# The experts' down weights issued from GpSimd's DMA queue instead of SyncE's, in a two-block transformer forward pass on one core

## The chip, the cores and the metric

The kernel runs on one NeuronCore of a Trainium2 chip. Times are device microseconds (us) of one launch. The span of a profile runs from the first to the last instruction of the profiled execution.

## The reference

Two transformer blocks of 256 tokens by 1024 features in float32 run one after the other. The first has four layers, each a mixer (forgetting attention, S5, pooling, forgetting attention) and a dense SwiGLU of width 2816. The second has two layers with a hybrid mixer; its first feed-forward is dense, its second is a mixture of eight experts of width 3584, and each token uses two of them:

```python
def swiglu_2(x, wg, wu, wd):
    return (jax.nn.silu(x @ wg) * (x @ wu)) @ wd

def moe_swiglu(x, router, wg, wu, wd):
    t = x.reshape(bsz * s, d)
    top_v, top_i = lax.top_k((t @ router).astype(jnp.float32), TOP_K)
    top_w = jax.nn.softmax(top_v, axis=-1)
    gate = jnp.sum(jax.nn.one_hot(top_i, N_EXPERTS) * top_w[..., None], axis=1)
    for e in range(N_EXPERTS):
        y = y + gate[:, e:e + 1] * swiglu_2(t, wg[e], wu[e], wd[e])
```

The change touches only how the weights of this mixture reach on-chip memory.

## The kernel before

Every engine has a hand-written program, and semaphores join them. SyncE (SP) issues nearly all loads of weights. GpSimd (POOL) does no arithmetic in the layers: it issues small loads of parameters, the last two of which are the scale and shift rows of the final layer norm (L958, 0.5 MB each, one descriptor of 4 KB per partition), after it has waited for version 13 of x (the rows after the last mixer's layer norm).

**The expert stage** runs from 1935 us to the end. It gathers up to 88 tokens for each expert. An expert has 14 chunks of 256 hidden features. A chunk is three pieces of weights: 1 MB of gate, 1 MB of up, 1 MB of down. There are four slots: three in `ring` and one in `arena` (`expert_slot`, L372). In each slot the first 4096 columns hold gate or up weights, the last 2048 the down weights. Gate and up are loaded for two chunks at a time: one DMA of 2 MB puts gate for both into the even slot, a second puts up for both into the odd slot. Such two chunks are called a pair here. A down DMA brings 1 MB for one chunk.

**TensorE's order** (L1743 to L1821) is `gate_up` of chunk c (L1762, 128 matmuls of 64 weight columns and 88 tokens), then `down` of chunk c-1 (L1778, 64 matmuls). Before the `gate_up` of an even slot it waits until both 2 MB DMAs have landed (`ex_loaded`, L1754); before a `down`, for its 1 MB (`ex_down_loaded`, L1771). The first matmul of the `down` that follows an odd slot's `gate_up` gives that pair's gate and up places back (`ex_released`, L1782); the last matmul of a `down` gives that down place back (`ex_down_released`, L1784). Twelve of an expert's chunks run in a hardware loop of three rounds with four chunks each (L1809); between two experts there are the output transposes (L1725), the gather for the next expert (L1710) and the scatter of the last result (L1737).

**SyncE's order** (`expert_chunk`, L534 to L550) is written out: for each chunk in turn, with an even slot first wait for `ex_released` and issue gate and up, then in either case wait for `ex_down_released` of the slot and issue down. All go to one hardware DMA queue, q1 in the profile, which spreads each DMA over the 16 DMA engines. The first four chunks wait instead for the ring slots that the last mixer still uses, and for version 13 of x for the slot in `arena` (`place_free`). POOL's DMAs go to another queue, q0; TensorE's own instructions are fetched in blocks of 16 KB through q8.

In a gate or up DMA a descriptor moves 2 KB (512 columns of float32); in a down DMA it moves 8 KB (two rows of 1024), so each engine has 64 descriptors of a gate or up DMA and 8 of a down DMA.

Of the kernel before, what the change touches and what calls it, by code (L numbers as in the profile page):

```python
# [12 lines left out]
D = 1024  # L13
# [10 lines left out]
N_EXP = 8  # L24
# [11 lines left out]
FC = 256  # L36
NSUB = FC // P
# [5 lines left out]
PASSES = -(-S // CAP)  # L43
# [142 lines left out]
def build(nc, inp, table, out):  # L186
# [3 lines left out]
    with ctx:  # L190
        def sb(name, shape, dt=F32):
            return ctx.enter_context(nc.sbuf_tensor(name, shape, dt))

        def sem(name):
            return ctx.enter_context(nc.semaphore(name))
# [170 lines left out]
        overflow = sb("overflow", [P, 1], I32)  # L366
        M_CH = F_EXP // FC
        M_RING = RING + 1
# [3 lines left out]
        def expert_slot(n):  # L372
            return ring[:, n, :] if n < RING else last_slot
# [19 lines left out]
        def x_at(ver):  # L393

            return (x_part, 4 * (ver - 1)) if 2 <= ver <= 9 else (x_ready, 1 if ver == 1 else ver - 8)
# [27 lines left out]
        ex_down_loaded = [sem(f"expert_down_loaded{i}") for i in range(RING + 1)]  # L423
        ex_released = [sem(f"expert_gate_up_released{i}") for i in range(RING + 1)]
        ex_down_released = [sem(f"expert_down_released{i}") for i in range(RING + 1)]
        rows_loaded = sem("row_vectors_loaded")
        rows_used = sem("row_vectors_used")
        overflow_ready = sem("overflow_flag_ready")
# [19 lines left out]
        def _(sp):  # L448
            t = Tally()
# [78 lines left out]
            def place_free(slot):  # L528
                if slot < RING:
                    sp.wait_ge(released[slot], t.count[f"released{slot}"] + 1)  # L530
                else:
                    sp.wait_ge(*x_at(13))

            def expert_chunk(gate, up, down, f0, first):  # L534

                n = t.up("expert_chunk") - 1
                slot = n % M_RING
                if slot % 2 == 0 and not first:
                    sp.wait_ge(ex_released[slot + 1], t.up(f"ex_released{slot + 1}"))
                if slot % 2 == 0:  # L540
                    for i, w in enumerate((gate, up)):
                        if first:
                            place_free(slot + i)
                        sp.dma_start(expert_slot(slot + i)[:, 0:4096].rearrange("p (k n) -> p k n", n=2 * FC),
                                     w.rearrange("(k p) n -> p k n", p=P)[:, :, bass.ds(f0, 2 * FC)])\
                          .then_inc(ex_loaded[slot], 16)
                if not first:
                    sp.wait_ge(ex_down_released[slot], t.up(f"ex_down_released{slot}"))
                sp.dma_start(expert_slot(slot)[:, 4096:6144].rearrange("p (s n) -> p s n", n=D),
                             down[bass.ds(f0, FC), :].rearrange("(p s) n -> p s n", s=NSUB)).then_inc(ex_down_loaded[slot], 16)  # L550

            def moe_pass(b):
                for e in range(N_EXP):
                    gate, up, down = (inp[k][0, e] for k in ("moe_w_gate_2", "moe_w_up_2", "moe_w_down_2"))
                    first = b == e == 0
                    for c in range(2 if not first else M_RING):
                        expert_chunk(gate, up, down, c * FC, first)
                    done = 0
                    if first:
                        for c in range(M_RING, 2 + M_RING):  # L560
                            expert_chunk(gate, up, down, c * FC, False)
                        done = 1
                    with sp.Fori(0, M_ROUNDS - done) as i:
                        adds = {f"ex_released{j}": 1 for j in range(1, M_RING, 2)}
                        adds.update({f"ex_down_released{j}": 1 for j in range(M_RING)})
                        adds["expert_chunk"] = M_RING
                        t.enter(i, M_ROUNDS - done, adds)
                        for j in range(M_RING):
                            expert_chunk(gate, up, down, i * (M_RING * FC) + (j + 2 + done * M_RING) * FC, False)
                        t.leave()  # L570

            moe_pass(0)
            sp.wait_ge(overflow_ready, 1)
            more = sp.value_load(overflow[0:1, 0:1], min_val=0, max_val=1)
            with sp.If(more > 0):
                for b in range(1, PASSES):
                    moe_pass(b)
# [359 lines left out]
        @block.gpsimd  # L937
        def _(pool):

            pool.wait_ge(x_ready, 1)  # L940
            n = 0
            br, bi = (inp[k][0].rearrange("g p c -> p g c") for k in ("s5_b_re", "s5_b_im"))
            cr, ci = (inp[k][0].rearrange("(k g) c p -> (g c) k p", g=GPT) for k in ("s5_c_re", "s5_c_im"))
            loads = [(b_own[0:64], br), (b_own[64:P], bi), (b_other[0:64], bi), (b_other[64:P], br),
                     (c_in[:, 0, :, 0:64], cr), (c_in[:, 0, :, 64:P], ci)]
            for half in (slice(0, 64), slice(64, P)):
                loads += [(lam_in[0:G5, 0, half], inp["s5_a_re"][0]), (lam_in[0:G5, 1, half], inp["s5_a_im"][0])]
            loads += [(dt5, inp["s5_log_dt"].broadcast_to([P, G5]))]
            for dst, src in loads:
                pool.dma_start(dst, src, allow_slow_non_contiguous=True).then_inc(s5_loaded, 16)  # L950
                n += 16
            assert n == S5_LOADS, n

            pool.dma_start(router.rearrange("p (k e) -> p k e", e=N_EXP),
                           inp["moe_router_2"][0].rearrange("(k p) e -> p k e", p=P)).then_inc(router_loaded, 16)

            def row(k, src):
                pool.dma_start(rowv[:, k, :], src.broadcast_to([P, D])).then_inc(rows_loaded, 16)  # L958
            pool.wait_ge(*x_at(4))
            pool.dma_start(arena[:, LATE_AT:LATE_AT + n_const - n_early], table[:, n_early:n_const]).then_inc(late_loaded, 16)  # L960
            row(0, inp["pool_b"])
            row(1, inp["pool_scale"])
            pool.wait_ge(*x_at(6))
            row(0, inp["final_norm_g"].rearrange("(o d) -> o d", o=1))
            for n, (wn, bn, l) in enumerate((("ln1_w_2", "ln1_b_2", 0), ("ln2_w_2", "ln2_b_2", 0),
                                             ("ln1_w_2", "ln1_b_2", 1), ("ln2_w_2", "ln2_b_2", 1))):
                pool.wait_ge(*x_at(10 + n))
                row(0, inp[wn][l:l + 1, :])
                row(1, inp[bn][l:l + 1, :])


        @block.tensor
        def _(pe):
# [724 lines left out]
            pe.wait_ge(late_loaded, 16)  # L1698
            hybrid(0, turn_z(0))
            tks = [tk for _, tk in turn_z(4)]  # L1700
            ffn(tks[0:2], tks[2:4], (), plain=False)
            hybrid(1, turn_z(0))
# [968 lines left out]
```

## Time and profile before

| | |
|---|---|
| median of 3 runs | 2904.29 us (2901.03 to 2906.14) |
| the profiled execution | 2901.52 us; span 2899.6 us |
| TensorE busy over the span | 2736.8 us, 94% |
| q1 | 606.13 MB |
| mean granted TensorE clock | 0.985 of full |

In the profile PE is TensorE's matmuls, PEld its weight loads (they overlap), SPq the issuing on SyncE's queue. An "idle" in brackets stands in front of the group beside which it is printed; "issue" is idle time for which no semaphore or DMA was found. Line numbers are those of the kernel before.

### The profile page before, as it was taken

Reading aid. Unit: us, or ns where it says so; the run is one execution under the profiler, and the core shown is the slowest. Engines: PE = TensorE matmul, PEld = TensorE weight load, DVE = VectorE, ACT = ScalarE, POOL = GpSimd, SP = SyncE. Lnnn points to the kernel's source line nnn. Section 1 sums busy time; section 2 is a strip of 40 time slices with the busy share of each in tenths; the row PEclk is TensorE's granted clock in tenths of the full one; section 3 lists DMA queues with packets and bytes.
Section 4 is the critical chain, followed back from the end, with each engine's and each line's share of the span. In section 5 each row is a group of like instructions: output and inputs, shape, how many; then the busy total and the mean of one; then the engine's idle time right before and its main releaser. Section 6 shows DMA issues by size and latency. Waiting matters only on the chain.

```text
span 2899.6 us, 79960 instructions
## 1 busy us (share of the span) xinstructions
PE 2736.8 (94%) x37718; PEld 2201.9 (76%) x37718; DVE 957.6 (33%) x1644; ACT 344.5 (12%) x717; POOL 18.5 (1%) x28
## 2 busy tenths in 40 slices
PE   8999998999899999999999999889999999979997
PEld 5677775677687775776657776569899998978987
DVE  1445444445645415544355343540000000000001
ACT  1210022100100003000240001510000000000000
POOL 1000000000000000000000000000000000000000
PEclk9999999999999999999999999999999999999998
DMA  7244413554434433354324543259999999997995
GB/s 223 89 144 141 164 59 118 182 175 158 170 129 139 171 132 110 124 175 146 115 102 148 173 161 130 102 192 384 371 396 377 381 392 366 395 373 281 382 382 209
DMA packets 307917, 620.55 MB, mean 214 GB/s; under 512 B 8886, under 2 KB 126908, under 8 KB 293212
## 3 DMA queue, kind: packets, MB, share of 16 engines
q1 hardware_dynamic: 304688, 606.13, 57.7%
q0 software_dynamic: 2400, 10.09, 1.1%
q8 instruction: 211, 3.46, 0.5%
q10 hardware_dynamic: 588, 0.63, 0.1%
q14 instruction: 30, 0.25, 0.0%
HBM read 615.77 MB, written 1.05 MB: 213 GB/s over the span
## 4 chain that ended last, share of the span: by engine, by line
PE 79%; DVE 9%; DMA 7%; issue 3%; ACT 1%; SPq 1%; DVEq 0%; ACTq 0%
PE ps L1762 19%; PE ps L1028 12%; PE ps L1187 12%; PE ps L1115 9%; PE ps L1778 9%; PE ps L1039 8%; DMA ring<-in_ffn_w_down 6%; PE ps L1677 2%; PE ps L1737 1%; PE ps L1710 1%; DVE arena L1912 1%; DVE ring L1911 1%; DVE arena L1910 1%; DVE arena L1913 1%; DVE arena L2065 1%
## 5 line engine op out<-in xcount | busy, mean ns | idle before, releaser
L1762 PE MATMUL ps<-arena,ring 128*64 128x88 f32 x10752 | 438.8, 240 | 29.7 <-issue 27.9
L1762 PEld LDWEIGHTS ps<-arena,ring 128*64 128x64 f32 x10752 | 423.4, 139 | 39.8 <-issue 37.6
L1115 PE MATMUL ps<-ring,arena 128*128 128x512 f32 x880 | 390.3, 597 | 0.0
L1028 PE MATMUL ps<-xT,ring 128*128 128x256 f32 (+2 forms) x1664 | 363.9, 380 | 2.2 <-DVE xT L1880 1.0
L1028 PEld LDWEIGHTS ps<-xT,ring 128*128 128x128 f32 (+2 forms) x1664 | 312.4, 188 | 55.9 <-issue 9.0
L2591 DVE TENSOR_TENSOR arena<-arena,ps 128x176 f32<-128x176 f32 x112 | 37.8, 338 | 844.6 <-ACT arena L899 844.6
L1115 PEld LDWEIGHTS ps<-ring,arena 128*128 128x128 f32 x880 | 163.2, 190 | 193.2 <-issue 193.1
L1778 PE MATMUL ps<-arena,ring 128*64 128x88 f32 x5376 | 224.0, 239 | 12.4 <-issue 12.4
L1778 PEld LDWEIGHTS ps<-arena,ring 128*64 128x64 f32 x5376 | 214.1, 137 | 13.2 <-issue 13.2
L1187 PEld LDWEIGHTS ps<-xT,ring 128*64 128x64 f32 x2816 | 158.1, 140 | 53.1 <-issue 53.1
L1187 PE MATMUL ps<-xT,ring 128*64 128x128 f32 x2816 | 167.9, 278 | 22.8 <-DVE arena L1997 16.6
L1910 DVE TENSOR_TENSOR arena<-ring 128x1024 f32<-128x1024 f32 x44 | 53.9, 1224 | 361.7 <-DMA ring<-in_ffn_w_down 361.7
L1187 PE MATMUL ps<-arena 128*64 128x128 f32 x2816 | 170.3, 273 | 0.0
L1187 PE MATMUL ps<-arena,ring 128*64 128x128 f32 x2816 | 162.0, 273 | 0.0
L1187 PEld LDWEIGHTS ps<-arena 128*64 128x64 f32 x2816 | 158.4, 137 | 0.0
L1762 PE MATMUL ps<-arena 128*64 128x88 f32 x3584 | 149.9, 239 | 7.2 <-issue 7.2
L1187 PEld LDWEIGHTS ps<-arena,ring 128*64 128x64 f32 x2816 | 156.1, 137 | 0.0
L1762 PEld LDWEIGHTS ps<-arena 128*64 128x64 f32 x3584 | 142.9, 138 | 9.1 <-issue 8.9
L643 ACT ACTIVATE arena<-arena 128x512 f32<-128x512 f32 x55 | 34.7, 630 | 945.7 <-DVE arena L2002 596.5
L899 ACT ACTIVATE arena<-ps 128x176 f32<-128x176 f32 x112 | 35.5, 317 | 824.1 <-PE ps L1762 824.1
L1039 PE MATMUL ps<-ring,xT 128*128 128x512 f32 (+1 forms) x320 | 131.7, 572 | 0.0
L1039 PE MATMUL ps<-ring,arena 128*128 128x512 f32 (+1 forms) x288 | 119.4, 576 | 3.2 <-ACT arena L718 3.2
(443 smaller groups left out, 2294.1 us busy)
## 6 DMA issues: line engine op xcount, KB each, us to landing
ring<-in_moe_w_gate SPq DMA_DIRECT2D x56, 2048.0 KB, 9.8
ring<-in_ffn_w_gate_up SPq DMA_DIRECT2D x88, 1024.0 KB, 7.5
ring<-in_moe_w_down SPq DMA_DIRECT2D x84, 1024.0 KB, 14.5
ring<-in_moe_w_up SPq DMA_DIRECT2D x28, 2048.0 KB, 14.2
arena<-in_moe_w_up SPq DMA_DIRECT2D x28, 2048.0 KB, 14.8
ring<-in_ffn_w_down SPq DMA_DIRECT2D x55, 1024.0 KB, 11.0
arena<-in_moe_w_down SPq DMA_DIRECT2D x28, 1024.0 KB, 10.2
ring<-in_fox_w_in SPq DMA_DIRECT2D x20, 768.0 KB, 6.1
```

The lines of the kernel that those rows point to most:

```text
L643: act.activation(g, g, ACT.Silu).then_inc(silu_ready, 1)
L899: act.activation(silu[:, par, 0:NSUB * CAP], ps[:, par, 0:NSUB * CAP], ACT.Silu).then_inc(silu_ready, 1)
L1028: ins = pe.matmul(o, lhsT=w[:, k, c0:c0 + m], rhs=rhs[:, k, :], start=(k == 0), stop=(k == kt - 1))
L1039: ins = pe.matmul(o, lhsT=lhs[:, k0 + k, i * P:(i + 1) * P], rhs=w[:, k, c0:c0 + n], start=(k == 0), stop=(k == kt - 1))
L1115: return pe.matmul(ps[:, 4 + 2 * i + h, :], lhsT=h_par[:, s * S + i * P:s * S + (i + 1) * P], rhs=w[:, s, h * 512:(h + 1) * 512], start=(c ...
L1187: ins = pe.matmul(o[h], lhsT=w_of[:, u, k, h], rhs=x_of[:, k, :], start=(k == 0), stop=(k == 3))
L1677: ins = pe.matmul(ps[:, b, :], lhsT=mixT[:, k, (b % 2) * P:(b % 2 + 1) * P], rhs=w[:, k, 0:512], start=(k == 2), stop=(k == 7), skip_group ...
L1710: ins = pe.matmul(ps[h, 6 + k // 4, (k % 4) * CAP:(k % 4 + 1) * CAP], lhsT=x[:, i, k * P + h.start:k * P + h.stop], rhs=perm[:, e, i, :], ...
L1762: ins = pe.matmul(ps[h, par, c0:c0 + CAP], lhsT=w[:, k, s, h], rhs=xe[:, k, :], start=(k == 0), stop=(k == KD - 1))
L1778: ins = pe.matmul(o[h], lhsT=w[:, s, m * P + h.start:m * P + h.stop], rhs=hid[:, par, s * CAP:(s + 1) * CAP], start=False, stop=False, ski ...
L1910: then(tt(t3, b22, b12, ALU.subtract))
L2591: dve.tensor_tensor(hid[:, par, 0:NSUB * CAP], silu[:, par, 0:NSUB * CAP], ps[:, par, NSUB * CAP:2 * NSUB * CAP], ALU.mult).then_inc(hid_r ...
```

## The change

SyncE now issues only gate and up. POOL, after its last layer-norm rows, runs a loop of its own over experts and chunks, waits for `ex_down_released` of the slot (not for the first four chunks), and issues the same down DMA with the same semaphore. Every other engine is as before.

```diff
-            def expert_chunk(gate, up, down, f0, first):
+            def expert_chunk(gate, up, f0, first):
...
-                if not first:
-                    sp.wait_ge(ex_down_released[slot], t.up(f"ex_down_released{slot}"))
-                sp.dma_start(expert_slot(slot)[:, 4096:6144].rearrange("p (s n) -> p s n", n=D),
-                             down[bass.ds(f0, FC), :].rearrange("(p s) n -> p s n", s=NSUB)).then_inc(ex_down_loaded[slot], 16)
...
@@ the end of the gpsimd block @@
                 row(0, inp[wn][l:l + 1, :])
                 row(1, inp[bn][l:l + 1, :])
+            t = Tally()
+
+            def expert_down(down, f0, first):
+                slot = (t.up("expert_chunk") - 1) % M_RING
+                if not first:
+                    pool.wait_ge(ex_down_released[slot], t.up(f"ex_down_released{slot}"))
+                pool.dma_start(expert_slot(slot)[:, 4096:6144].rearrange("p (s n) -> p s n", n=D),
+                               down[bass.ds(f0, FC), :].rearrange("(p s) n -> p s n", s=NSUB))\
+                    .then_inc(ex_down_loaded[slot], 16)
+
+            def moe_pass(b):
+                for e in range(N_EXP):
+                    down = inp["moe_w_down_2"][0, e]
+                    head = 2 + M_RING if b == e == 0 else 2
+                    for c in range(head):
+                        expert_down(down, c * FC, b == e == 0 and c < M_RING)
+                    with pool.Fori(0, (M_CH - head) // M_RING) as i:
...
+                        for j in range(M_RING):
+                            expert_down(down, i * (M_RING * FC) + (j + head) * FC, False)
...
+            moe_pass(0)
+            pool.wait_ge(overflow_ready, 1)
+            more = pool.value_load(overflow[0:1, 0:1], min_val=0, max_val=1)
+            with pool.If(more > 0):
...
```

## Rows read from the trace of the kernel before

**Rows 1.** Stretches: busy us of PE, PEld, DVE, ACT, POOL; clock, DMA share, GB/s
```profile
1940.00:1950.00 10.00, 10.00 (x236) 9.35 (x234) 1.00 (x5) 1.66 (x4) 0.00 (x0) 1.00 0.06 23
...
2190.00:2200.00 10.00, 9.15 (x236) 8.88 (x234) 0.67 (x2) 0.37 (x2) 0.00 (x0) 1.00 0.80 295
...
2240.00:2250.00 10.00, 10.00 (x271) 10.00 (x267) 0.34 (x1) 0.32 (x1) 0.00 (x0) 1.00 1.03 404
```
**Rows 2.** Waits from 1800 us on: us in total, times, longest us
```profile
PE ps L1762 <- issue: 35.0, 23, 7.6
...
PE ps L1762 <- DMA arena<-in_moe_w_up: 0.8, 1, 0.8
```
**Rows 3.** A stall of PE in the third expert's first loop round
```profile
2213.31 1.81 PE L1762 MATMUL ps<-arena,ring 128*64 128x88 f32 x41 [1.14 <-issue]
```
**Rows 4.** The instruction queue from 2190 to 2216 us, then from 2216 to 2280 us
```profile
q8 instruction: 5, 0.08, 1.4%
...
q8 instruction: 1, 0.02, 0.1%
```
**Rows 5.** Order of time on SyncE's queue, third expert: start us, us, DMA
```profile
2232.29 1.37 SPq L549 DMA_DIRECT2D ring<-in_moe_w_down  x1
2239.57 0.35 SPq L549 DMA_DIRECT2D arena<-in_moe_w_down  x1
2244.50 0.38 SPq L544 DMA_DIRECT2D ring<-in_moe_w_gate  x1
2244.97 0.85 SPq L544 DMA_DIRECT2D ring<-in_moe_w_up  x1
```
**Rows 6.** DMAs issued at 2232.29, 2239.57, 2244.97: size, us to landing (last number)
```profile
ring<-in_moe_w_down SPq DMA_DIRECT2D x1, 1024.0 KB, 14.8
arena<-in_moe_w_down SPq DMA_DIRECT2D x1, 1024.0 KB, 10.0
ring<-in_moe_w_up SPq DMA_DIRECT2D x1, 2048.0 KB, 15.4
```
**Rows 7.** Order of time on PE, third expert: start us, us, matmuls
```profile
2244.01 2.66 PE L1778 MATMUL ps<-arena,ring 128*64 128x88 f32 x64
...
2260.99 5.09 PE L1762 MATMUL ps<-arena,ring 128*64 128x88 f32 x128
```
**Rows 8.** First expert's tightest pair: up's issue, its landing, the `gate_up` that needs it
```profile
2014.59 1.34 SPq L544 DMA_DIRECT2D ring<-in_moe_w_up  x1
...
ring<-in_moe_w_up SPq DMA_DIRECT2D x1, 2048.0 KB, 15.9
...
2030.62 5.04 PE L1762 MATMUL ps<-arena,ring 128*64 128x88 f32 x128
```
**Rows 9.** Last expert's tightest pair: the same three
```profile
2842.77 0.53 SPq L544 DMA_DIRECT2D arena<-in_moe_w_up  x1
...
arena<-in_moe_w_up SPq DMA_DIRECT2D x1, 2048.0 KB, 15.8
...
2858.80 2.66 PE L1762 MATMUL ps<-arena,ring 128*64 128x88 f32 x64
```
**Rows 10.** The first of POOL's last two DMAs before the change, in order of time
```profile
1925.81 0.53 POOL L958 DMA_DIRECT2D arena<-in_ln_w  x1 [153.39 <-DVE x_rows L2388]
```
**Rows 11.** The first expert's first `down`, in order of time on PE
```profile
1949.25 2.60 PE L1778 MATMUL ps<-arena,ring 128*64 128x88 f32 x64
```
**Rows 12.** DMA queues in 1929:1930 (one line), 1930:1931, 1931:1932 (two lines each)
```profile
q0 software_dynamic: 1, 0.00, 1.0%
...
q0 software_dynamic: 58, 0.24, 57.9%
q1 hardware_dynamic: 91, 0.19, 47.9%
...
q0 software_dynamic: 66, 0.26, 66.6%
q1 hardware_dynamic: 65, 0.13, 39.0%
```

More of the change, by code:

```diff
@@ L546, in expert_chunk @@
                           .then_inc(ex_loaded[slot], 16)
-                if not first:
-                    sp.wait_ge(ex_down_released[slot], t.up(f"ex_down_released{slot}"))
-                sp.dma_start(expert_slot(slot)[:, 4096:6144].rearrange("p (s n) -> p s n", n=D),
-                             down[bass.ds(f0, FC), :].rearrange("(p s) n -> p s n", s=NSUB)).then_inc(ex_down_loaded[slot], 16)
             def moe_pass(b):
                 for e in range(N_EXP):
-                    gate, up, down = (inp[k][0, e] for k in ("moe_w_gate_2", "moe_w_up_2", "moe_w_down_2"))
+                    gate, up = (inp[k][0, e] for k in ("moe_w_gate_2", "moe_w_up_2"))
                     first = b == e == 0
                     for c in range(2 if not first else M_RING):
-                        expert_chunk(gate, up, down, c * FC, first)
+                        expert_chunk(gate, up, c * FC, first)
                     done = 0
@@ L560, in moe_pass @@
                         for c in range(M_RING, 2 + M_RING):
-                            expert_chunk(gate, up, down, c * FC, False)
+                            expert_chunk(gate, up, c * FC, False)
                         done = 1
@@ L564, in moe_pass @@
                         adds = {f"ex_released{j}": 1 for j in range(1, M_RING, 2)}
-                        adds.update({f"ex_down_released{j}": 1 for j in range(M_RING)})
                         adds["expert_chunk"] = M_RING
@@ L568, in moe_pass @@
                         for j in range(M_RING):
-                            expert_chunk(gate, up, down, i * (M_RING * FC) + (j + 2 + done * M_RING) * FC, False)
+                            expert_chunk(gate, up, i * (M_RING * FC) + (j + 2 + done * M_RING) * FC, False)
                         t.leave()
@@ L969, in _ @@
                 row(1, inp[bn][l:l + 1, :])
+            t = Tally()
[13 more added lines that the diff above has]
+                    with pool.Fori(0, (M_CH - head) // M_RING) as i:
+                        adds = {f"ex_down_released{j}": 1 for j in range(M_RING)}
+                        adds["expert_chunk"] = M_RING
+                        t.enter(i, (M_CH - head) // M_RING, adds)
+                        for j in range(M_RING):
+                            expert_down(down, i * (M_RING * FC) + (j + head) * FC, False)
+                        t.leave()
+            moe_pass(0)
+            pool.wait_ge(overflow_ready, 1)
+            more = pool.value_load(overflow[0:1, 0:1], min_val=0, max_val=1)
+            with pool.If(more > 0):
+                for b in range(1, PASSES):
+                    moe_pass(b)
         @block.tensor
```

## The prediction

> **What bounds the kernel now.** The change acts only in the expert stage, from 1935 us on, so I read that stage alone. First its stretches of 10 us: in the steady part of an expert TensorE is busy for all 10.00 us and the DMA engines too, share 1.03 at 404 GB/s; just after an expert's start the DMA share falls to 0.80, because all slots are full [rows 1]. Then the waits: TensorE waited for weights once, 0.8 us; its other idle time, 35.0 us in 23 pieces before `gate_up`, has no semaphore [rows 2]. A typical piece is 1.14 us in the middle of a block of matmuls [rows 3], and such pieces lie where the instruction queue is at work: 5 fetches in the 26 us of the first loop round, 1 in the next 64 us [rows 4]. So TensorE bounds the stage by its matmuls and its instruction fetches, and the DMA engines are a very close second.
>
> How close shows in one pair of chunks. The pair's last DMA, up, was issued at 2244.97 and took 15.4 us [rows 5, 6], so it landed at 2260.4; `gate_up` needed it at 2260.99 [rows 7]. Slack 0.6 us. The two downs ahead of it landed at 2232.29 + 14.8 = 2247.1 and 2239.57 + 10.0 = 2249.6 [rows 5, 6]. So the engines spend 2.5 us on a down and 10.8 us on gate and up together: 15.8 us per pair, while TensorE uses a pair in 14.56 us (six blocks of 64 matmuls; seven of them lie between the starts at 2244.01 and 2260.99 [rows 7], 2.43 us each). The DMA side loses about 1.2 us per pair and makes it good at the next expert's start. The tightest pair of each expert, by the same subtraction: 0.1 us of slack in the first [rows 8], then 0.7, 0.6, 0.0 (the wait of 0.8 us in [rows 2]), 0.5, 2.0 (there a 7.6 us stall [rows 2] let the slots fill), 0.4, and 0.2 in the last [rows 9]. Sum 4.5 us over eight.
>
> A down has far more time. It is released at the end of one `down` and wanted eleven blocks of 64 matmuls later, 11 x 2.43 = 26.7 us; it takes 10.0 to 14.8 us [rows 6]. **Gate and up are urgent, down is not**, and one queue in order of issue happens to serve them so.
>
> **Part 1: SyncE loses 112 down DMAs and their waits.** Gain taken: nothing. SyncE sat in a wait for a down, but its next gate was never late for that: `down` at 2244.01 released the pair and the gate went out at 2244.50 [rows 5, 7]. The wait that ended last was TensorE's release. Bounds: at best the 0.8 us of waiting for weights, at worst nothing.
>
> **Part 2: POOL issues 112 downs.** A POOL DMA keeps it for 0.53 us [rows 10], 59 us in all, spread over 950 us in which it has nothing else to do; one down falls due per 7.28 us. Register work and loop branches come on top and are hidden likewise. Behind its waits nothing is queued but more downs.
>
> **Part 3: the first four downs are queued behind POOL's wait for version 13 and two layer-norm loads.** They go out at about 1925.81 + 2 x 0.53 = 1926.9 and later. From then on the engines owe the last up (2 MB), four downs (4 MB) and 1 MB of layer-norm rows: 7.3 million bytes at 404 GB/s [rows 1] are 18 us, so all lands by about 1946. The first down is wanted at 1949.25 [rows 11]. Before, the engines lay empty in 1940 to 1950, share 0.06 [rows 1]; that hole is the cover. Cost 0; with the cover gone it would be at most those 18 us.
>
> **Part 4: the order of service.** This is where the time goes. With both queues loaded the engines alternate packet by packet: 66 of q0 against 65 of q1 in one us, 58 against 91 in the us before, when q0 was just starting [rows 12]. A packet of q0 was there 4 KB, of q1 2 KB. A packet of a down is 8 KB, of gate or up 2 KB. One for one, a down takes four fifths of the engines: its 8 packets per engine go by while gate or up gets 8 of its 128. **A down thus overtakes**, and the pair in front of it lands 2.5 us later. It does so only after a lag: the POOL DMA of 1925.81 had moved one packet by 1930 [rows 10, 12], 4.2 us after its issue.
>
> Does it arrive in time to overtake? In the tight pair the first down is released when the block of 2244.01 ends, 2246.6 [rows 7], and starts 4.2 us later at 2250.8: surely before up lands at 2260.4. The second is released 7.28 us after the first, starts at 2258.1, and with the first in front up lands at 2262.9: it too overtakes. When TensorE already waits for weights, the second release is late as well. Counted from one pair's landing, the second down starts 7.3 + 4.2 = 11.5 us on and the next up would land at 10.8 + 2.5 = 13.3 us. A margin of under 2 us, of which the landing's own tail may take half. So I count both downs, 5.0 us, in six experts and one, 2.5 us, in two.
>
> The delay is paid once per expert, at its tightest pair: total bytes are the same, and the next start refills the slots. Six times 5.0 plus two times 2.5 is 35.0 us; less the slacks, 4.5 us, is **30.5 us**. Bounds: 0 if no down overtakes, 35.5 if both always do (8 x 5.0 - 4.5). I stay near the upper end because the one stretch in which both queues were loaded shows one for one.
>
> The Trainium skill ("DMA: Bandwidth & Descriptors", section "Issuing engines are not separate DMA queues") says that DMAs from any engine run on the same 16 DMA engines and interleave, and that several issuers save only issue time. By that alone the sum would be 0, since no issue time is on the path; the shares of 1.03 agree that there is no bandwidth to win. Interleaving that leaves the sum of bytes alone still changes who lands first.
>
> **Part 5: the joint rate and the fetches.** Mixed, the two queues moved 0.43 and 0.39 MB per us [rows 12], against 0.404 (404 GB/s) unmixed [rows 1]: from 6% faster to 4% slower. Over the 4 pairs before the tightest, some 6.5 us of each mixed (twice 8 packets of 10 KB per engine, 1.3 MB), that is -1.5 to +1 us per expert. I take 0, nearest their mean. A fetch of TensorE's instructions now stands in turn with two queues. No row shows that; bounds from [rows 2]: all 35.0 us of idle gone, or doubled. I take 0, because the amount of data ahead of it in the engines is the same.
>
> **Sum.** The profiled execution took 2901.5 us; 2901.5 + 30.5 = 2932. That execution stands 2.8 us below the median of the runs shown, 2904.29. About 0.2%, 6 us, is what a measurement of this kernel can tell from no change.
>
> **Rivals.**
> A. *Both downs mostly overtake* (forecast): 2932, and up to 2937 by its bound. Chance 0.54.
> B. *Only the first down overtakes*, because the second starts after up's last packets: 8 x 2.5 - 4.5 = 15.5 us, 2917. For it: the margin under 2 us. Against: the tight pair's own times. Chance 0.16.
> C. *Nobody waits*: q0's lag grows with what q1 has queued, and downs come in behind the pair as before. 2902, within the noise. For it: a single stretch shows the alternation under 2 KB packets. Against: 4.2 us was seen with q1 loaded. The skill's rule above would give this. Chance 0.13.
> D. *Faster*. The fetch of a block of instructions waits behind what q1 holds in the engines. If downs in a queue of their own shorten that, the pauses of 1.14 us shrink; half of the 35.0 us is 17.5, so 2884. It decides from the point where a 16 KB fetch takes no longer than the 4.85 us in which TensorE uses it up; now it takes about 4.85 + 1.14. Against: bytes in flight stay the same, and less catching up at the starts leaves less slack later. Chance 0.06.
> E. *Slower still: fetches also wait their turn behind 8 KB packets of a second queue*: the 35.0 us double, on top of A: 2967. For it: a third queue to alternate with. Against: one more packet is 8 KB, beside some 100 KB ahead in each engine (4.2 us at a sixteenth of 404 GB/s). Chance 0.11.
>
> **How the numbers follow.** A is likeliest: 2932. Low end 2902 keeps B and half of C and leaves out D, 0.12 in all. High end 2960 takes A with the worse rate (8 us) and part of E, leaving out about 0.08. Slower by over 0.2%: A, B, E, 0.81; within: C, 0.13; faster: D, 0.06.
>
> **What would show it.** Right: TensorE waits for `in_moe_w_gate` or `in_moe_w_up` at two or three pairs near each expert's end, 3 to 5 us per expert; downs land in some 8 us instead of 10 to 15, ups of tight pairs in 18 to 20 instead of 15 to 17; DMA share below 1 for longer after each start; POOL shows 112 more issues of about 0.53 us; the stage before 1935 us is unchanged. Wrong: downs still landing in 10 us or more with ups as before (C), or the "issue" idle before L1762 far from 35 us (D, E), or waits for the down weights themselves, which I hold impossible at this slack.

## The result

| | median | ratio to before, 95% interval |
|---|---|---|
| before, 4 runs beside it | 2902.66 us | |
| changed | 2931.14 us (2922.84 to 2948.35, 4 runs) | 1.0101 [1.0065, 1.0137] |
| changed, measured again | 2937.18 us (2933.54 to 2938.61, 4 runs) | 1.0119 [1.0104, 1.0134] |

The change costs 28 to 34 us, about 1%. The forecast was 2932.0.

The page of the changed kernel, its sums and queues:

```profile
span 2931.4 us, 80054 instructions
...
PE 2743.9 (94%) x37718; PEld 2207.6 (75%) x37718; DVE 957.1 (33%) x1644; ACT 344.9 (12%) x717; POOL 77.6 (3%) x140
...
q1 hardware_dynamic: 288560, 488.68, 47.3%
q0 software_dynamic: 18528, 127.54, 11.0%
```

PE was busy 2736.8 us before and is now 2743.9: the span grew by 31.8 us, PE's work by 7.1. q1 gave 117.4 MB to q0: the 112 downs. POOL gained 59.1 us, which is 112 x 0.53.

The waits of the changed kernel in the expert stage, 1900 to 2940 us (L1787 was L1762, L1803 was L1778), which answer to [rows 2]:

```profile
PE ps L1787 <- issue: 30.2, 21, 7.7
PE ps L1787 <- DMA ring<-in_moe_w_up: 15.6, 12, 2.3
PE ps L1787 <- DMA arena<-in_moe_w_up: 15.5, 10, 2.7
...
PE ps L1803 <- issue: 10.5, 12, 1.4
```

TensorE now waits 31.1 us for up, in 22 pieces, where it waited 0.8 us in one. It never waits for a down. Its idle time without a releaser fell by 8.5 us (`down` had 14.2 us of it before, `gate_up` 35.0). In the same window PE is busy 930.91 us against 922.98. 30.3 - 8.5 + 7.9 is 29.7 of the 31.8 us.

The DMA issues on the same page, size and median time to landing (last number):

```profile
ring<-in_moe_w_gate SPq DMA_DIRECT2D x56, 2048.0 KB, 11.3
...
ring<-in_moe_w_down POOLq DMA_DIRECT2D x84, 1024.0 KB, 8.4
ring<-in_moe_w_up SPq DMA_DIRECT2D x28, 2048.0 KB, 18.8
arena<-in_moe_w_up SPq DMA_DIRECT2D x28, 2048.0 KB, 18.7
...
arena<-in_moe_w_down POOLq DMA_DIRECT2D x28, 1024.0 KB, 7.7
```

Before, these medians were 9.8 (gate), 14.5 (down), 14.2 and 14.8 (up), 10.2 (down). Downs land 2.5 to 6 us sooner, though TensorE never waited for them; ups land 4 to 5 us later, and TensorE waits for them.

One pair, in the third expert. First SyncE's and POOL's issues, then PE, in order of time (us, us, instruction; the idle time before it in brackets):

```profile
2238.37 0.37 SPq L544 DMA_DIRECT2D ring<-in_moe_w_gate  x1
2238.83 0.53 SPq L544 DMA_DIRECT2D arena<-in_moe_w_up  x1
...
2241.16 0.53 POOL L971 DMA_DIRECT2D ring<-in_moe_w_down  x1 [6.77 <-PE ps L1803]
2248.53 0.53 POOL L971 DMA_DIRECT2D arena<-in_moe_w_down  x1 [6.84 <-PE ps L1803]
```

```profile
2257.88 3.91 PE L1787 MATMUL ps<-arena,ring 128*64 128x88 f32 x64 [2.74 <-DMA arena<-in_moe_w_up]
2261.57 3.04 PE L1787 MATMUL ps<-arena 128*64 128x88 f32 x64
2264.44 2.60 PE L1803 MATMUL ps<-arena,ring 128*64 128x88 f32 x64
```

The up issued at 2238.83 took 19.0 us and landed at 2257.8. Two downs were issued behind it and landed 8.4 and 7.8 us after their issues, at 2249.6 and 2256.3: both were carried in front of its tail. The queues in the single us 2247:2248, while the first of them was on its way (packets, MB, share of 16 engines' time):

```profile
q0 software_dynamic: 43, 0.35, 84.9%
q1 hardware_dynamic: 37, 0.07, 18.4%
```

Nearly as many packets of one as of the other, 8 KB against 2 KB: the down gets 0.35 of the 0.42 MB. In 2112:2113 it was 47 against 45.

### The profile page after: what moved, and what is told of

The parts are those of the page before. It is cut to its first block, busy times and chain, and to the rows that moved or that the text cites. A ratio compares the mean times of both kernels' runs of the same rounds, so it can differ in the third digit from the quotient of the medians.

```text
span 2931.4 us, 80054 instructions
## 1 busy us (share of the span) xinstructions
PE 2743.9 (94%) x37718; PEld 2207.6 (75%) x37718; DVE 957.1 (33%) x1644; ACT 344.9 (12%) x717; POOL 77.6 (3%) x140
## 4 chain that ended last, share of the span: by engine, by line
PE 69%; DMA 17%; DVE 9%; issue 2%; ACT 1%; SPq 1%; DVEq 0%; ACTq 0%
PE ps L1787 14%; PE ps L1053 12%; PE ps L1212 12%; PE ps L1140 9%; PE ps L1064 8%; DMA ring<-in_moe_w_up 6%; DMA ring<-in_ffn_w_down 6%; PE ps L1803 5%; DMA arena<-in_moe_w_up 4%; PE ps L1702 2%; PE ps L1762 1%; PE ps L1735 1%; DVE arena L1935 1%; DVE ring L1936 1%; DVE arena L1937 1%
## 5 line engine op out<-in xcount | busy, mean ns | idle before, releaser
L1787 PE MATMUL ps<-arena,ring 128*64 128x88 f32 x10752 | 443.7, 242 | 55.5 <-issue 23.4
L1787 PEld LDWEIGHTS ps<-arena,ring 128*64 128x64 f32 x10752 | 426.7, 140 | 69.0 <-issue 32.8
L1803 PE MATMUL ps<-arena,ring 128*64 128x88 f32 x5376 | 222.1, 239 | 9.2 <-issue 8.9
L1803 PEld LDWEIGHTS ps<-arena,ring 128*64 128x64 f32 x5376 | 212.4, 137 | 11.2 <-issue 11.1
L1787 PE MATMUL ps<-arena 128*64 128x88 f32 x3584 | 148.8, 240 | 6.8 <-issue 6.8
L1787 PEld LDWEIGHTS ps<-arena 128*64 128x64 f32 x3584 | 142.2, 139 | 8.3 <-issue 8.1
## 6 DMA issues: line engine op xcount, KB each, us to landing
arena<-in_moe_w_up SPq DMA_DIRECT2D x28, 2048.0 KB, 18.7
```

Of the source, the lines that this page charges most:

```text
L1787: ins = pe.matmul(ps[h, par, c0:c0 + CAP], lhsT=w[:, k, s, h], rhs=xe[:, k, :], start=(k == 0), stop=(k == KD - 1))
L1803: ins = pe.matmul(o[h], lhsT=w[:, s, m * P + h.start:m * P + h.stop], rhs=hid[:, par, s * CAP:(s + 1) * CAP], start=False, stop=False, ski ...
```

## The experiments

My theory: what costs the time is the **order of service**. The engines serve the two queues by turns, a down's packets are four times as large, and so each down passes the up that TensorE needs. Rivals: the software queue is slow in itself; the instruction fetches suffer; something other than the order differs.

**1. The change again.**

> The changed kernel once more, unchanged, as the anchor of this group. Both theories: 2931 us, 1.010 of the kernel before, within some 8 us. TensorE waits some 31 us for up weights in 20 or more pieces.

2937.18 us, ratio 1.0119 [1.0104, 1.0134]; TensorE waited 32.8 us for up, in 24 pieces. The loss is real.

**2. Everything of the experts on POOL's queue, in the order of the kernel before.** One queue again, but the software one. (The last two layer-norm rows go out behind the first four chunks here, not ahead of them.)

```diff
-                        sp.dma_start(expert_slot(slot + i)[:, 0:4096].rearrange("p (k n) -> p k n", n=2 * FC),
+                        pool.dma_start(expert_slot(slot + i)[:, 0:4096].rearrange("p (k n) -> p k n", n=2 * FC),
...
-                sp.dma_start(expert_slot(slot)[:, 4096:6144].rearrange("p (s n) -> p s n", n=D),
+                    pool.dma_start(expert_slot(slot)[:, 4096:6144].rearrange("p (s n) -> p s n", n=D),
```

> Gate, up and down of all experts go through POOL's queue, in the order that SyncE had before: software-made descriptors for everything, but one queue, so no down can overtake. Theory 'order' (two queues alternate packet by packet, so downs overtake gate and up): the loss goes, 2903 to 2915 us, the upper end if POOL's later first packet costs the tight pairs up to 1.5 us each (8 x 1.5 = 12). Rival 'software queue' (the queue that POOL feeds is itself slower or disturbs the engines): three times as many bytes go through it, so at least the 2931 us of the change, and with the loss in proportion about 2990. Downs land in 13 us or more again under the first.

2912.07 us (2905.08 to 2920.76, 9 runs), 1.0033 [1.0020, 1.0047]. Its waits:

```profile
PE ps L1765 <- issue: 37.7, 26, 6.8
...
PE ps L1765 <- DMA ring<-in_moe_w_up: 2.5, 4, 1.1
PE ps L1765 <- DMA arena<-in_moe_w_up: 1.6, 3, 0.8
```

All 352 MB of the experts' weights go over the software queue, and TensorE has only 4.1 us of waits for up; its ups land in 14.5 and 14.6 us, as in the kernel before. The software queue costs 0.3%, a third of the change's loss at most. What the change lost it lost by having two queues.

**3 and 4. Both queues, but POOL holds its downs back**: until its pair's gate and up have landed (3), or its gate alone (4, with a semaphore of its own, on which TensorE then waits too). The edit of 3:

```diff
+                even = slot - slot % 2
+                landed = t.up(f"ex_loaded{even}", 32) if slot % 2 == 0 else t.value(f"ex_loaded{even}")
                 if not first:
+                    pool.wait_ge(ex_loaded[even], landed)
                     pool.wait_ge(ex_down_released[slot], t.up(f"ex_down_released{slot}"))
```

> The changed kernel, but POOL issues a down only once both gate and up of its own pair have landed: same queue, same descriptors, same bytes, the order of before restored. Theory 'order': 2905 to 2920 us; the part above 2903 is the gap between the landing of up and the first packet of the down, about 2 us per pair where nothing else is queued. Ups of tight pairs land in 15 to 17 us again. Rival 'software queue': 2931 us, as the queue carries the same.

> As the one before, but POOL waits only for gate of the pair, not for up. POOL's lag of 4.2 us then lies beside the 5.4 us in which up lands, so the downs start about when up ends. Theory 'order': 2901 to 2912 us, at or below the one before. Rival 'software queue': 2931 us.

Hold for both: 2912.81 us (2910.39 to 2925.86, 6 runs), 1.0036 [1.0023, 1.0048]. Hold for gate: 2907.97 us (2886.87 to 2917.35, 12 runs), 1.0009 [0.9991, 1.0027]. The waits with the gate held:

```profile
PE ps L1793 <- issue: 30.5, 22, 6.8
...
PE ps L1793 <- DMA arena<-in_moe_w_up: 6.6, 6, 3.1
PE ps L1793 <- DMA ring<-in_moe_w_up: 4.0, 4, 1.7
```

The downs are still on POOL's queue and still land fast (7.3 and 9.2 us), and two thirds of the waits for up are gone, 31.1 to 10.6 us; ups land in 16.1 and 15.9 us. Holding POOL back, which adds only a semaphore to TensorE's work, takes back some nine tenths of the loss: this is the strongest single piece for the order. Holding until up has landed is a little worse in its median. The likely reason, not shown, is that the down is then issued only some 18.6 us after its pair and runs beside the next pair. Its profiled execution was its slowest, 2925.86 us, with 29.2 us of waits for up and ups landing in 18.6 and 18.7 us (I had expected 15 to 17), so this trace does not show the order restored and is not its typical run.

**5 and 6. One half of the change each**: only the first down of a pair on POOL's queue (shown), or only the second (0 and 1 exchanged).

```diff
@@ GpSimd @@
+                if slot % 2 in (0,):
                     if not first:
                         pool.wait_ge(ex_down_released[slot], t.up(f"ex_down_released{slot}"))
...
@@ SyncE @@
+                if slot % 2 in (1,):
+                    if not first:
+                        sp.wait_ge(ex_down_released[slot], t.up(f"ex_down_released{slot}"))
...
```

> Only the first down of each pair goes over POOL's queue; the second stays on SP's, behind its pair's up, as before. If the loss is made by overtaking, one 8 KB-packet down of 2.5 us in front of each up costs about half of the change's loss: 15 us, 2911 to 2923 beside 2903 for the kernel before, with waits for up of 10 to 18 us in the expert stage. Rival (the loss comes from having two queues loaded at all, whatever is in the second): nearly the whole loss, 2928 or more. Rival (only the second down matters, since it is the one that meets a late up): within 3 us of the kernel before.

> Only the second down of each pair goes over POOL's queue; the first stays on SP's, behind its pair's up. If both downs overtake, as my forecast said, this loses about as much as the other half: 10 to 18 us, 2911 to 2923. If only the first down overtakes, because the second starts after up's last packets, it stays within 3 us of the kernel before, 2903. The two halves together should give the change's whole loss, 28 to 34 us; if they give clearly less, the two overtakings feed each other.

| on POOL's queue | median (5 runs each) | ratio | loss |
|---|---|---|---|
| first down of a pair | 2917.80 us | 1.0042 [1.0028, 1.0056] | 13.8 us |
| second down | 2920.58 us | 1.0052 [1.0038, 1.0066] | 16.6 us |
| sum | | | 30.4 us |
| both (the change) | | | 28 to 34 us |

TensorE waited 12.2 us for up with the first down on POOL's queue, 16.0 us with the second, against 31.1 with both. Each of the two overtakes, each costs about the same, and they add up. My rival B, only the first down overtakes, is out, and so is a cost of two loaded queues as such, which one half would have shown nearly whole.

**7. Queues exchanged**: gate and up on POOL's, downs on SyncE's.

```diff
@@ SyncE @@
-                        sp.dma_start(expert_slot(slot + i)[:, 0:4096].rearrange("p (k n) -> p k n", n=2 * FC),
+                    sp.dma_start(expert_slot(slot)[:, 4096:6144].rearrange("p (s n) -> p s n", n=D),
@@ GpSimd @@
-                pool.dma_start(expert_slot(slot)[:, 4096:6144].rearrange("p (s n) -> p s n", n=D),
+                        pool.dma_start(expert_slot(slot + i)[:, 0:4096].rearrange("p (k n) -> p k n", n=2 * FC),
```

> Queues exchanged against the change: gate and up on POOL's queue, downs on SP's. If the engines alternate packet by packet whichever queue it is, downs overtake again and at once, without the software queue's lag of about 4 us, while gate and up now have that lag: up waits of 30 us or more, 2935 to 2950. If the loss of the change came from a priority of the software queue over the hardware queue, gate and up now have it: DMA waits under 5 us and 2903 to 2914, as the run with everything on POOL's queue.

2952.21 us (2947.37 to 2958.68, 5 runs), 1.0180 [1.0162, 1.0198]: 2 us above my range, in the direction of the theory. Its waits, then its queues in the us 2250:2251:

```profile
PE ps L1796 <- DMA arena<-in_moe_w_up: 26.3, 14, 3.5
PE ps L1796 <- DMA ring<-in_moe_w_up: 23.6, 15, 2.4
PE ps L1796 <- issue: 21.1, 21, 2.1
```

```profile
q1 hardware_dynamic: 40, 0.33, 80.9%
q0 software_dynamic: 32, 0.12, 30.9%
```

Neither queue is seen to have priority: whichever carries the downs' 8 KB packets takes most of the bytes. Here q0's packets are 4 KB each (0.12 MB in 32): POOL's queue carried these rows of 2 KB in packets of 4 KB, so gate and up even got twice the share per turn, and still lost. Why the loss, 48 us, is larger than the change's was not taken apart; the downs now start without POOL's lag, and the software queue itself cost 9 us in run 2.

**8. Each down cut into two DMAs of half the columns**, rows of 2 KB in place of 8 KB, still on POOL's queue.

```diff
-                pool.dma_start(expert_slot(slot)[:, 4096:6144].rearrange("p (s n) -> p s n", n=D),
-                               down[bass.ds(f0, FC), :].rearrange("(p s) n -> p s n", s=NSUB))\
+                for h in range(2):
+                    cols = slice(h * 512, (h + 1) * 512)
+                    pool.dma_start(expert_slot(slot)[:, 4096:6144].rearrange("p (s n) -> p s n", n=D)[:, :, cols],
+                                   down[bass.ds(f0, FC), cols].rearrange("(p s) n -> p s n", s=NSUB))\
...
-                        pe.wait_ge(ex_down_loaded[slot], t.up(f"ex_down_loaded{slot}", 16))
+                        pe.wait_ge(ex_down_loaded[slot], t.up(f"ex_down_loaded{slot}", 32))
```

> All downs on POOL's queue as in the change, but each as two DMAs with packets of 2 KB in place of 8 KB. If the engines serve the two queues packet by packet, a down then has half of the engines and not four fifths while gate or up is in flight: it lands in 9 to 12 us in place of 8.4, up in 16 to 18 in place of 18.8, and since a down that takes longer still passes ahead of the tail of up only in part, the loss shrinks to 10 to 22 us: 2913 to 2925. If the queues are served byte by byte, or the software queue has priority, nothing changes: 2931 to 2938.

2928.88 us (2925.13 to 2937.08, 5 runs), 1.0087 [1.0072, 1.0102]: above my range. The waits:

```profile
PE ps L1789 <- DMA ring<-in_moe_w_up: 26.1, 14, 2.9
PE ps L1789 <- issue: 18.0, 20, 2.0
PE ps L1805 <- issue: 10.5, 14, 1.5
PE ps L1789 <- DMA arena<-in_moe_w_up: 10.0, 8, 2.7
```

The queues in the us 2248:2249, while a down and an up were both on their way:

```profile
q0 software_dynamic: 63, 0.26, 67.3%
q1 hardware_dynamic: 62, 0.13, 35.4%
```

A miss, and a useful one. Its condition was not met: the 0.26 MB in 63 packets are 4 KB each, not 2 KB, since POOL's queue again put two rows of 2 KB into one packet, as in run 7. So a down had two thirds of the bytes, not half; the two queues still took turns packet by packet. Down's share fell from four fifths to two thirds, and the waits for up did not shrink (36.1 us); up lands in 19.3 and 18.4 us, as in the change. I had overlooked what the prediction's own numbers say: a down starts while 9.6 us (first) or some 4.8 us (second) of its pair are still to come, 3.9 or 1.9 MB, and even at half the engines its 1 MB would be through before up is. **A down that finishes first delays up by its whole size, whatever its share per turn**: that is my reading, seen for packets of 8 and of 4 KB; none of 2 KB was run on POOL's queue.

The ratio is 1.0087 for 1.0101 and 1.0119. The intervals overlap, so it is not shown that this run gained on the change at all; if it did, the 4 to 9 us lie in the "issue" lines, 28.5 us for 40.7: the piece of over 7 us is gone. Where from, runs 9 to 12 were made to tell.

**9 and 10. Gate held and each down cut in two**: the edits of 4 and 8 together, so packets of 4 KB on POOL's queue again, measured twice, beside other runs of the kernel before.

> POOL waits for the pair's gate, as in the run that did so before, and its downs have packets of 2 KB. In that run 10.6 us of waits for up were left, since a down still passed an up in flight at four packets of bytes to one. By the packet rule the small packets take most of those away: 0 to 5 us of waits for up, and 2893 to 2903 against 2903 for the kernel before and 2908 for the run with the wait alone. If packet size is nothing to it: 2905 to 2911. If the wait alone had settled the order and the rest was noise: no difference from 2908.

> The run with the gate wait and 2 KB packets once more, beside new runs of the kernel before: 2893 to 2898 if the gain of 0.2 to 0.3 per cent is real, 2900 to 2906 if it was chance.

2895.63 us, 0.9980 [0.9962, 0.9998], and 2897.94 us, 0.9984 [0.9972, 0.9995]: faster than the kernel before by 0.2%, for the first time, with intervals that end just below 1. Waits for up 5.5 us, "issue" 33.8 us with no piece over 1.6 (run 9).

**11. The kernel before with each down cut in two**: the edit of 8 on SyncE's queue, where the packets are 2 KB indeed; nothing on POOL's.

> The kernel before with one thing of the fast run: each down as two DMAs with 2 KB packets, still on SP's queue. Two readings of why the run with the gate wait and small packets took 2895.6 us against 2904.0. One: the order of service is now as good as before and what it gained is the two fetch stalls of the sixth expert, 7.6 and 5.3 us in the kernel before, which its profile does not have, because the instructions lie elsewhere; then this kernel, which is also two instructions longer per down in SP's program only, either keeps its stalls and stays at 2901 to 2907, or loses them and goes to 2885 to 2895. Two: 2 KB packets of a down in themselves are carried better; then the landings of gate and up shrink by some 0.5 us or more and TensorE's 7.6 us stall stays.

2894.25 us (2887.84 to 2899.78, 12 runs), 0.9971 [0.9962, 0.9981]. It **beats both kernels**; run 10 beside it stands 3.7 us higher, with overlapping intervals. The waits:

```profile
PE ps L1765 <- issue: 22.9, 23, 1.5
PE ps L1781 <- issue: 11.3, 11, 1.8
PE ps L1765 <- DMA ring<-in_moe_w_up: 3.0, 3, 1.5
PE ps L1765 <- DMA arena<-in_moe_w_up: 2.1, 3, 0.8
```

Against the kernel before: "issue" 35.5 us (with 1.3 us on another line) for 49.2, waits for up 5.1 for 0.8. So this is not better service: ups land in 15.7 and 16.2 us, later than before. What went are two stalls of the sixth expert, 12.9 us together. The two profiled executions differ by only 4.3 us of span where the medians differ by 9.8 (one was faster than its median, the other slower), so the traces account for a part of the gain. PE in the kernel before, and the instruction queue from 2540 to 2660 us there; then that queue in run 11:

```profile
2592.94 2.66 PE L1778 MATMUL ps<-arena,ring 128*64 128x88 f32 x64
2603.20 0.55 PE L1762 MATMUL ps<-arena,ring 128*64 128x88 f32 x3 [7.60 <-issue]
2609.03 3.20 PE L1762 MATMUL ps<-arena,ring 128*64 128x88 f32 x40 [5.28 <-issue]
```

```profile
q8 instruction: 17, 0.28, 1.0%
```

```profile
q8 instruction: 10, 0.16, 0.6%
```

Seven more blocks of instructions were fetched there. Over the whole program the page counts 211 fetches in the kernel before, and 211 in the change, in 1 to 6; it counts 202 in 7 to 12. The count follows neither the waits nor the order of service; it goes with the program. All eight profiles with 211 have the pair of long stalls in the sixth expert, 6.8 us or more and some 5; none with 202 has it.

**12. Run 11 with 8 KB packets**: the same two DMAs and waits, cut by partitions in place of columns (the tile and the weights both sliced by `half`).

```diff
-                    cols = slice(h * 512, (h + 1) * 512)
+                    half = slice(h * 64, (h + 1) * 64)
```

> The kernel before with each down as two DMAs on SP's queue, as in the run before_small (2894), but cut by partitions, so that the packets stay at 8 KB: the same instructions and waits as before_small, only the packet size is that of the kernel before. If the two long stalls of the sixth expert (7.6 and 5.3 us) went away because the programs are longer and the instructions lie elsewhere, they are gone here too and this takes 2890 to 2898. If they went away because a fetch of instructions waits behind fewer bytes when a down has 2 KB packets, they are back and this takes 2901 to 2907. I hold the first for somewhat likelier, 0.6.

3327.81 us (3316.94 to 3331.98, 5 runs), 1.1452 [1.1430, 1.1473]: neither reading had this. The waits, then the queue from 2400 to 2402 us, when a half down was on its way:

```profile
PE ps L1765 <- DMA ring<-in_moe_w_up: 179.5, 24, 10.7
PE ps L1765 <- DMA arena<-in_moe_w_up: 152.6, 24, 8.3
PE ps L1781 <- issue: 21.0, 7, 5.4
```

```profile
DMA packets 70, 0.40 MB, mean 198 GB/s; under 512 B 15, under 2 KB 15, under 8 KB 24
...
q1 hardware_dynamic: 70, 0.40, 101.7%
```

A DMA into 64 of the 128 partitions kept all engines busy and moved half: 198 GB/s where whole ones moved 404 [rows 1]. For the question asked: the fetches were 202 again with 8 KB packets, and no pair of 7 and 5 us came, which speaks for the program and against the packet size. But its "issue" idle reaches 5.4 us in other places and its timing is another throughout, so I call the cause likely, not shown. Run 7 says the same from the other side: 8 KB packets, 202 fetches, no piece over 2.1 us.

With that, the versions fall in two families, and the order of service costs about the same in each (the packets of the downs are 8 KB on the left, 2 or 4 KB on the right):

| | 211 fetches | 202 fetches |
|---|---|---|
| one hardware queue | 2903 to 2905 (before) | 2894.25 (11) |
| two queues, gate held | 2907.97 (4) | 2895.63, 2897.94 (9, 10) |
| two queues, free | 2931.14, 2937.18 (change, 1) | 2928.88 (8) |
| free less one queue | 28 to 34 us | 34.6 us |

## Why the prediction was right, point by point

**Part 1**, SyncE relieved, gain nothing: right. What SyncE waits for before gate and up is still TensorE's release (54 waits, as before), and nothing was gained.

**Part 2**, POOL's 59 us hidden: right, 59.1 us, and TensorE waits nowhere for POOL or for a down.

**Part 3**, first four downs behind the layer-norm rows, cost 0: right. POOL in the changed kernel:

```profile
1926.98 0.53 POOL L953 DMA_DIRECT2D arena<-in_ln_b  x1
1927.50 1.57 POOL L971 DMA_DIRECT2D ring<-in_moe_w_down  x3
1929.06 0.53 POOL L971 DMA_DIRECT2D arena<-in_moe_w_down  x1
```

TensorE started the stage at 1936.22 for 1935.53 us and did not wait for those downs.

**Part 4**, the order of service: right in mechanism and, in sum, in size. Forecast 30.5 us of waits for up, measured 31.1 - 0.8 = 30.3. Packets one for one (37 and 45 of q1 against 43 and 47 of q0), a lag of POOL's DMAs near 4 us (the down of 2248.53 shows up in q0 only from 2252 on, 24 packets in 2252:2253), both downs overtaking (runs 5, 6). By experts TensorE waited 4.7, 2.3, 3.7, 5.1, 4.0, 1.1, 5.7 and 4.6 us, where I had forecast 5.0 or 2.5 less the slack. The shape was off: I put one payment at each expert's tightest pair, and it comes in one to four pieces of 0.2 to 2.7 us, in pairs that I had thought to have slack. And what I held of packet size was too strong: a down takes four fifths of the engines, that is seen, but in run 8 it took two thirds and the loss was no smaller for it.

The Trainium skill ("DMA: Bandwidth & Descriptors", section "Issuing engines are not separate DMA queues") was the ground of rival C. The trace agrees that there was no bandwidth to win: the changed kernel moves 402 GB/s from 2110 to 2120 us, the kernel before 404 [rows 1]. But its last step, that only issue time is at stake, does not hold here: who is served first was worth 1%.

**Part 5**, joint rate 0, fetches 0. The fetches were a mis-sized term: "issue" idle fell by 8.5 us in the changed kernel. Perhaps a part of it now passes under the waits for data; that is not shown. A term I did not have at all stands against it, +7.9 us of PE's busy time, in this execution mostly lower clock (see the last section). They cancel within 1 us, which is luck and not reckoning. In run 1 the same terms are 32.0 us of waits, -7.6 of "issue" and +5.9 of busy time, of which lower clock is only 1.7 and the rest is not named. The forecast of 2932.0 stands 0.9 us from the first median and 5 from the second; the second, with 21 runs of the kernel before beside it, is the surer ratio. The sum also started from an execution 2.8 us under its median, 2904.29; from the median it would give 2934.8, so 0.9 us flatters it.

**The rivals.** B (2917) is out by runs 5 and 6, C (nobody waits) by the first four lines of waits, E (fetches double) by the lower "issue" lines. D, faster by shorter fetch pauses, was out for the change; yet some 10 us were probably to be had from fetches (run 11), by another way than its own.

## What to carry to other kernels

Here a second DMA queue brought no bandwidth (402 GB/s for 404); it brought a second place in the line, and traffic that could wait passed traffic that could not. Where one queue in order of need is nearly saturated, keep it, or make the less urgent queue wait on a landing of the urgent one (here gate's, with up still to land: 28 to 34 us lost without the wait, some 3 to 5 with it). Before a version a few us faster is believed, look whether the instruction fetches moved: here a mere change in the program's text went with 10 us, a third of the effect studied, and the fetches are its likely cause.

## What the runs showed of the hardware that I had not expected

**Half a down's partitions, half the rate** (run 12): 198 GB/s at an engine share of 101.7%. The Trainium skill ("DMA: Bandwidth & Descriptors", section "Rules for kernel authors") advises against two transfers to disjoint partition halves, since both use the same 16 engines and serialize. By that alone the halves would have cost nothing beyond a second DMA; measured, they cost 14.5%. So the advice holds, and more was lost than serializing gives. Why the rate halves, no run here shows.

**Some waits also cost clock.** In the lines of the pair in the third expert, after a wait of 2.74 us, 64 matmuls took 3.91 us, the next 3.04, then 2.60 again. The stretch 2257:2262 of the changed kernel has a granted clock of 0.71, that of the 5 us ahead of it 1.00:

```profile
2252.00:2257.00 5.00, 3.14 (x84) 2.96 (x79) 0.34 (x1) 0.32 (x1) 0.53 (x1) 1.00 1.02 401
2257.00:2262.00 5.00, 4.12 (x70) 4.12 (x72) 0.00 (x0) 0.00 (x0) 0.00 (x0) 0.71 1.06 410
```

That is a share of the time at 1.2 GHz and the rest at 2.4. In this execution it came after four of the five waits of 2 us or more (2.01, 2.74, 2.19, 2.35, not after 2.44), at 1.6 to 1.8 us each against 5.08 us for 128 matmuls or 2.60 to 2.65 for 64: 6.7 of PE's 7.9 us of added busy time. The length of the wait does not decide it. In run 1, the same kernel, it came after one of three (2.56 us, 1.7 us lost), and the longest wait of all was followed by 128 matmuls at full pace:

```profile
2381.91 5.08 PE L1787 MATMUL ps<-arena,ring 128*64 128x88 f32 x128 [3.21 <-DMA ring<-in_moe_w_up]
```

The forecast had priced a wait at its own length only; what it costs on top was 6.7 us in one execution and 1.7 in the other.

**The number of fetches went with the programs' text.** 211 or 202 fetches of 16 KB; in run 7, with 202, no line of TensorE's program differs from the kernel before. Two executions of version 4 took 2886.87 and 2890.43 us, 18 to 21 us under its median, as if the long stalls had been missing; no profile of such an execution was taken, and that stays open.
